# Moving the high part of each weight slot by 128 bytes in a 14-stage float32 kernel on one core

## The chip, the cores and the metric

The kernel runs on one core of a Trainium2 chip. The metric is the device time of one execution in microseconds (us). Before the change it is 2582.13 us, the median of 3 runs (2581.76 to 2582.37). Smaller is better.

## The reference

The program takes 256 tokens of width 1024 through two blocks, 14 stages in all. Every stage ends with a residual sum and a layer norm. All arithmetic is float32. Cut to what matters here:

```python
def first_block(x, ...):                 # two layers
    for layer in range(2):
        h = hybrid_mixer(x, ...)         # x @ w_in, gating, gated linear attention, @ w_out
        x = layer_norm(ALPHA * x + h, ...)
        f = swiglu(x, ...) if layer % 2 == 0 else moe_swiglu(x, ...)   # 8 experts, top 2
        x = layer_norm(ALPHA * x + f, ...)

def second_block(x, mem, ...):           # two layers
    for i in range(2):
        x = layer_norm_2(ALPHA * x + 0.5 * swiglu_2(x, gate, up, down), ...)
        x = layer_norm_2(ALPHA * x + (mixer_ab if i % 2 == 0 else mixer_c)(x, ...), ...)
        x = layer_norm_2(ALPHA * x + memory_attn(x, mem, ...), ...)
        x = layer_norm_2(ALPHA * x + 0.5 * swiglu_2(x, gate, up, down), ...)
```

`swiglu(x)` is `(silu(x @ w_gate) * (x @ w_up)) @ w_down`. Nearly all the arithmetic is products of the 256 tokens with large weight matrices.

## The kernel before, in words

**Split products.** Outside the expert stage, each float32 product is made of three products of float32r tiles. A value is split into a high part (rounded) and a low part (the rest). `product` (lines 581 to 583) issues them in this order: stationary high with moving high, stationary high with moving low, stationary low with moving high. I call such a group of three a triple.

**Two ways round.** In a plain block the tokens are the stationary operand (128 x 128) and the weights stream past as the moving operand, 512 columns at a time. The page writes it `bank<-part_hi,x_hi`, moving operand first. In a turned block the weights are stationary and 256 tokens are moving: `bank<-x_hi,turned_part_hi`. The stationary operand of a plain block is `x_hi`/`x_lo` (the stage's input), `cat_hi`/`cat_lo` (input of an output projection), `hT_hi`/`hT_lo` (hidden units of a feed-forward) or `mem_hi`/`mem_lo`.

**The ring.** Weights pass through a ring of 9 slots in SBUF. A slot holds one block of 128 x 2048 float32 as it arrives (`raw`, 8192 bytes of each partition), and beside it another 8192 bytes. ScalarE rounds the block into the second half (`part_hi`, line 548). VectorE then subtracts and writes the low part over the raw block (`part_lo`, line 556). TensorE reads both parts. For a turned block the same slot is used through a second set of views, whose names begin with `turned_`. In the expert stage (the middle of the program) there is no split: each half of a slot holds raw weights, `raw` and `raw_hi`, and plain float32 matmuls read them as the moving operand (lines 1203, 1217, 1250, 1272).

**Order.** The order of the work on each engine is written out by hand. Slots are given out by the order in which earlier blocks are used up (`Ring.place`); the three mixers with their own buffers above slot 6 use slots 0 to 5 only. In the first stage the blocks 0, 1, 2, 3 of `w_in` lie in slots 0, 1, 2, 3, and TensorE takes 12 matmuls (4 triples) from a slot before it goes to the next.

**Addresses.** `x_at` is the address of `x_hi`, a multiple of 128 bytes. `place_memory` puts each view at the next address that stands in a chosen relation to it modulo 128 (`at_place`).

Of the kernel before, what the change touches and what calls it, by code (L numbers as in the profile page):

```python
# [5 lines left out]
P = 128  # L6
F32 = mybir.dt.float32
F32R = mybir.dt.float32r
# [38 lines left out]
SLOT = 2048  # L47
LINE = 128
APART = 64
# [89 lines left out]
class Program:  # L139
# [34 lines left out]
    def place_memory(self):  # L174
        nc = self.nc
        base = (nc.sbuf_base + 31) // 32 * 32
        at = [base]
# [7 lines left out]
        def over(name, shape, dt, offset):  # L185
            return nc.alloc_sbuf_tensor_at(name, shape, dt, offset=offset)

        x_at = at[0] = (at[0] + LINE - 1) // LINE * LINE
# [26 lines left out]
        self.vstats = put("gating_stats", [P, TT, GM_HEADS, 8])  # L215
        self.att_stats = put("softmax_stats", [P, 16, 3, TT])
        self.raw, self.part_hi, self.part_lo, self.raw_hi = ([[], []] for _ in range(4))
        at[0] = (at[0] + LINE - 1) // LINE * LINE
        for i in range(RING):
            if i == MIX_RING:  # L220
                arena = at[0]
            raw_at, hi_at = at[0], at[0] + 4 * SLOT + APART
            at[0] = hi_at + 4 * SLOT + APART
            for name, turned in (("", 0), ("turned_", 1)):
                at_place = lambda first: first + (x_at + turned * APART - first) % LINE
                self.raw[turned].append(over(f"{name}raw{i}", [P, SLOT], F32, at_place(raw_at)))
                self.part_lo[turned].append(over(f"{name}part_lo{i}", [P, SLOT], F32R, at_place(raw_at)))
                self.raw_hi[turned].append(over(f"{name}raw_hi{i}", [P, SLOT], F32, at_place(hi_at)))
                self.part_hi[turned].append(over(f"{name}part_hi{i}", [P, SLOT], F32R, at_place(hi_at)))
        at[0] = (at[0] + LINE - 1) // LINE * LINE  # L230
        silu_at = at[0]
        self.silu = [put(f"silu{i}", [P, FC]) for i in range(2)]
        self.h = [put(f"h{i}", [P, FC]) for i in range(2)]
# [2578 lines left out]
```

## Time and profile before

| | |
|---|---|
| median of 3 runs | 2582.13 us |
| the profiled execution, its own time | 2579.98 us |
| its span, first to last instruction | 2578.7 us |
| TensorE matmul busy | 2524.8 us, 98% |
| TensorE weight load busy | 1788.1 us |
| VectorE, ScalarE, GpSimd busy | 1054.1, 820.6, 144.4 us |
| HBM traffic | 248 GB/s over the span |
| granted TensorE clock, mean | 0.996 |

A matmul row's duration covers its way through the array, so neighbouring matmuls overlap. The duration is not what one matmul costs in a row of them. The distance from the start of one to the start of the next is, and the timeline gives starts to 0.01 us. Over several triples that resolves a nanosecond or two of each.

### The profile page before, as it was taken

What the parts mean: (1) busy time and instruction counts of PE and PEld (TensorE: products, weight loads), DVE (VectorE), ACT (ScalarE), POOL (GpSimd) and SP (SyncE); (2) the same over time, 40 slices, a digit from 0 to 9 for tenths busy, and PEclk for the clock granted to TensorE, in tenths of its full rate; (3) what the DMA queues carried; (4) which work ended last, traced back from release to release, by engine and by line L of the source; (5) the groups of instructions that cost most, each with busy time, mean ns of one, the idle gap of its engine ahead of it and who ended that gap; (6) DMA issues with size and microseconds to landing.
All of it is one profiled execution on the core that took longest, in us unless ns stands there. A gap on an engine that the chain in (4) does not pass through costs nothing.

```text
span 2578.7 us, 40653 instructions
## 1 busy us (share of the span) xinstructions
PE 2524.8 (98%) x18155; PEld 1788.1 (69%) x18155; DVE 1054.1 (41%) x1488; ACT 820.6 (32%) x1138; POOL 144.4 (6%) x143
## 2 busy tenths in 40 slices
PE   8999999999999999999999999999999999899998
PEld 6899885444444444444448987797988988688897
DVE  5755562010101000010116558646546545655554
ACT  5444342110101101010114436454444444634442
POOL 2200120000000000000000001000000004400000
PEclk9999999999999999999999999999999999999999
DMA  7565458999999999999985544446546546264651
GB/s 259 199 214 188 161 212 338 371 360 382 380 361 370 393 375 356 376 390 355 377 297 193 188 142 147 142 153 212 196 163 197 195 158 250 69 210 164 216 187 55
DMA packets 335286, 641.51 MB, mean 249 GB/s; under 512 B 15620, under 2 KB 128432, under 8 KB 334976
## 3 DMA queue, kind: packets, MB, share of 16 engines
q1 hardware_dynamic: 330000, 618.64, 66.5%
q0 software_dynamic: 5104, 20.20, 2.3%
q8 instruction: 144, 2.36, 0.4%
q14 instruction: 38, 0.31, 0.0%
HBM read 637.72 MB, written 1.05 MB: 248 GB/s over the span
## 4 chain that ended last, share of the span: by engine, by line
PE 91%; DVE 4%; POOL 2%; ACT 1%; DMA 1%; issue 0%; SPq 0%; DVEq 0%
PE bank L581 17%; PE bank L583 17%; PE bank L582 17%; PE bank L1203 15%; PE bank L1217 8%; PE bank L1250 7%; PE bank L1272 4%; DVE part_lo L556 1%; PE bank L977 1%; PE bank L1235 1%; PE bank L948 1%; PE bank L593 1%; POOL bias L2488 1%; PE bank L1189 1%; DVE x_rows L1833 1%; ACT part_hi L548 1%
## 5 line engine op out<-in xcount | busy, mean ns | idle before, releaser
L556 DVE TENSOR_TENSOR part_lo<-raw,part_hi 128x2048 fp32r<-128x2048 f32 x153 | 348.3, 2291 | 169.5 <-ACT part_hi L548 169.3
L581 PE MATMUL bank<-x_hi,turned_part_hi 128*128 128x256 f32 x1440 | 401.4, 279 | 0.0
L583 PE MATMUL bank<-x_hi,turned_part_lo 128*128 128x256 f32 x1440 | 399.1, 277 | 0.0
L582 PE MATMUL bank<-x_lo,turned_part_hi 128*128 128x256 f32 x1440 | 398.8, 277 | 0.0
L548 ACT ACTIVATE part_hi<-raw 128x2048 fp32r<-128x2048 f32 x153 | 289.1, 1908 | 14.9 <-DMA raw<-in_mem_w_kv_dram 6.9
L581 PEld LDWEIGHTS bank<-x_hi,turned_part_hi 128*128 128x128 f32 x1440 | 270.5, 188 | 4.1 <-issue 1.0
L582 PEld LDWEIGHTS bank<-x_lo,turned_part_hi 128*128 128x128 f32 x1440 | 270.3, 188 | 3.4
L583 PEld LDWEIGHTS bank<-x_hi,turned_part_lo 128*128 128x128 f32 x1440 | 270.8, 188 | 0.0
L556 DVE TENSOR_TENSOR turned_part_lo<-turned_raw,turned_part_hi 128x2048 fp32r<-128x2048 f32 x98 | 223.4, 2310 | 90.5 <-ACT turned_part_hi L548 89.9
L1203 PE MATMUL bank<-raw,expert_in 128*64 128x512 f32 x896 | 214.1, 598 | 0.0
L581 PE MATMUL bank<-part_hi,x_hi 128*128 128x512 f32 x528 | 213.2, 404 | 0.6 <-DVE x_lo L1781 0.5
L1203 PE MATMUL bank<-raw_hi,expert_in 128*64 128x512 f32 x896 | 211.2, 592 | 0.0
L2332 DVE TENSOR_TENSOR h<-silu,bank 128x256 f32<-128x256 f32 x56 | 23.6, 421 | 457.9 <-ACT silu L1742 457.9
L583 PE MATMUL bank<-part_hi,x_lo 128*128 128x512 f32 x528 | 208.4, 395 | 0.0
L582 PE MATMUL bank<-part_lo,x_hi 128*128 128x512 f32 x528 | 208.2, 394 | 0.0
L548 ACT ACTIVATE turned_part_hi<-turned_raw 128x2048 fp32r<-128x2048 f32 x98 | 183.3, 1908 | 4.6 <-DMA turned_raw<-in_c_w_in_dram 4.0
L581 PE MATMUL bank<-part_hi,hT_hi 128*128 128x512 f32 x440 | 173.1, 393 | 1.2 <-DVE hT_lo L1781 0.9
L582 PE MATMUL bank<-part_lo,hT_hi 128*128 128x512 f32 x440 | 172.6, 392 | 0.0
L583 PE MATMUL bank<-part_hi,hT_lo 128*128 128x512 f32 x440 | 172.5, 392 | 0.0
L1384 ACT ACTIVATE silu<-bank 128x256 f32<-128x256 f32 x110 | 42.3, 385 | 361.2 <-PE bank L583 361.2
L1203 PEld LDWEIGHTS bank<-raw_hi,expert_in 128*64 128x64 f32 x896 | 64.2, 137 | 128.0 <-issue 128.0
L2341 DVE TENSOR_TENSOR h<-silu,bank 128x128 f32<-128x128 f32 x56 | 16.1, 287 | 332.0 <-ACT silu L1752 332.0
(272 smaller groups left out, 3505.5 us busy)
## 6 DMA issues: line engine op xcount, KB each, us to landing
raw<-in_exp_w_gate_dram SPq DMA_DIRECT2D x112, 512.0 KB, 6.3
raw<-in_exp_w_up_dram SPq DMA_DIRECT2D x112, 512.0 KB, 7.2
raw_hi<-in_exp_w_gate_dram SPq DMA_DIRECT2D x112, 512.0 KB, 8.0
raw_hi<-in_exp_w_up_dram SPq DMA_DIRECT2D x112, 512.0 KB, 8.7
raw<-in_exp_w_down_dram SPq DMA_DIRECT2D x56, 1024.0 KB, 12.2
raw_hi<-in_exp_w_down_dram SPq DMA_DIRECT2D x56, 1024.0 KB, 13.7
raw<-in_ffn_w_down_dram SPq DMA_DIRECT2D x55, 1024.0 KB, 5.0
turned_raw<-in_ffn_w_gate_dram SPq DMA_DIRECT2D x70, 512.0 KB, 4.2
```

Of the source, the lines that this page charges most:

```text
L548: p.nc.scalar.activation(p.part_hi[t][i][:, :], p.raw[t][i][:, :], ACT.Copy).then_inc(*self.rounded.step((name,)))
L556: p.nc.vector.tensor_tensor(p.part_lo[t][i][:, :], p.raw[t][i][:, :], p.part_hi[t][i][:, :].bitcast(F32), ALU.subtract).then_inc(*self.spl ...
L581: nc.tensor.matmul(out, stat_hi, move_hi, start=start, stop=False, skip_group_check=True)
L582: nc.tensor.matmul(out, stat_hi, move_lo, start=False, stop=False, skip_group_check=True)
L583: return nc.tensor.matmul(out, stat_lo, move_hi, start=False, stop=stop, skip_group_check=True)
L593: mm = nc.tensor.transpose(p.bank[bank][:, k * P:(k + 1) * P], src[:, k * P:(k + 1) * P], p.const("identity"))
L948: mm = nc.tensor.matmul(p.bank[4 + i % 2][:, qt * T:(qt + 1) * T], q[:, qt * P:(qt + 1) * P], k, start=(j == 0), stop=(j == len(terms) - 1 ...
L1203: mm = p.nc.tensor.matmul(p.bank[4][half * PAIR:(half + 1) * PAIR, :].rearrange("p (m n) -> p m n", m=2), xe[:, kk, 0:PAIR], w[:, k, :, ha ...
L1217: mm = p.nc.tensor.matmul(p.bank[5][f * FOUR:(f + 1) * FOUR, 0:256].rearrange("p (m n) -> p m n", m=2), xe[:, kk, PAIR:SLOTS], w[:, k, :, ...
L1250: mm = p.nc.tensor.matmul(p.bank[0][half * PAIR:(half + 1) * PAIR, :], p.hT[:, j, d * PAIR:(d + 1) * PAIR], w[:, j, half * 512:(half + 1) ...
L1272: mm = p.nc.tensor.matmul(p.bank[1][f * FOUR:(f + 1) * FOUR, 0:256], p.hT[:, 2, tile * FOUR:(tile + 1) * FOUR], w[:, j, f * 256:(f + 1) * ...
L1384: nc.scalar.activation(p.silu[k % 2][:, :], p.bank[4 + k % 2][:, 0:FC], ACT.Silu).then_inc(*p.s.step(("silu", st, k)))
```

## The change

The number of instructions, their kinds, shapes and order are the same on every engine. Only start addresses of the unturned `raw_hi` and `part_hi` views change. Per slot, with A the slot's first address (slot i begins at A0 + 16512 i, before and after):

| view | before | after |
|---|---|---|
| `raw`, `part_lo` | A | A |
| `raw_hi`, `part_hi` | A + 8320 | A + 8192 |
| `turned_raw`, `turned_part_lo` | A + 64 | A + 64 |
| `turned_raw_hi`, `turned_part_hi` | A + 8256 | A + 8256 |

So before, the plain views were 65 lines of 128 bytes apart and the turned ones 64; after, both are 64. All else in memory stays where it was. Worked out from the allocation, counted in lines of 128 bytes: A0 = 63104 is line 493, so A is an odd line in the slots 0, 2, 4, 6, 8 and an even line in 1, 3, 5, 7. The stationary operands `x_hi`, `x_lo`, `cat_hi`, `cat_lo`, `mem_hi`, `mem_lo` begin at odd lines (`x_hi` at 16512 is line 129), `hT_hi` and `hT_lo` at even ones, and each 128 x 128 block in them begins a multiple of 512 bytes further on.

```diff
-        at[0] = (at[0] + LINE - 1) // LINE * LINE
+        at[0] += (x_at - at[0]) % LINE
         for i in range(RING):
             if i == MIX_RING:
                 arena = at[0]
-            raw_at, hi_at = at[0], at[0] + 4 * SLOT + APART
-            at[0] = hi_at + 4 * SLOT + APART
-            for name, turned in (("", 0), ("turned_", 1)):
-                at_place = lambda first: first + (x_at + turned * APART - first) % LINE
-                self.raw[turned].append(over(f"{name}raw{i}", [P, SLOT], F32, at_place(raw_at)))
-                self.part_lo[turned].append(over(f"{name}part_lo{i}", [P, SLOT], F32R, at_place(raw_at)))
-                self.raw_hi[turned].append(over(f"{name}raw_hi{i}", [P, SLOT], F32, at_place(hi_at)))
-                self.part_hi[turned].append(over(f"{name}part_hi{i}", [P, SLOT], F32R, at_place(hi_at)))
-        at[0] = (at[0] + LINE - 1) // LINE * LINE
+            for turned, name in enumerate(("", "turned_")):
+                raw_at = at[0] + turned * APART
+                hi_at = raw_at + 4 * SLOT
+                self.raw[turned].append(over(f"{name}raw{i}", [P, SLOT], F32, raw_at))
+                self.part_lo[turned].append(over(f"{name}part_lo{i}", [P, SLOT], F32R, raw_at))
+                self.raw_hi[turned].append(over(f"{name}raw_hi{i}", [P, SLOT], F32, hi_at))
+                self.part_hi[turned].append(over(f"{name}part_hi{i}", [P, SLOT], F32R, hi_at))
+            at[0] += 8 * SLOT + LINE
         silu_at = at[0]
```

`P` is 128, `SLOT` 2048 elements, `LINE` 128 and `APART` 64 bytes.

## Rows read from the trace of the kernel before

**Rows 1.** The page, the chain that ended last, by engine.
```profile
PE 91%; DVE 4%; POOL 2%; ACT 1%; DMA 1%; issue 0%; SPq 0%; DVEq 0%
```
**Rows 2.** Stretches before, in and behind the expert stage: length, then busy by engine.
```profile
0.00:420.00 420.00, 403.51 (x2412) 345.80 (x2413) 248.97 (x367) 186.75 (x199) 61.13 (x65) 1.00 0.63 216
420.00:1370.00 950.00, 947.72 (x8442) 412.11 (x8437) 103.70 (x216) 100.83 (x247) 2.29 (x4) 1.00 0.96 363
1370.00:2578.70 1208.70, 1173.55 (x7307) 1030.19 (x7306) 701.42 (x906) 533.02 (x692) 81.02 (x75) 0.99 0.51 170
```
**Rows 3.** Timeline of TensorE, first stage, slot 0 then slot 1: start, duration (us).
```profile
27.43 0.39 PE L581 MATMUL bank<-part_hi,x_hi 128*128 128x512 f32 x1
...
30.17 0.40 PE L581 MATMUL bank<-part_hi,x_hi 128*128 128x512 f32 x1
...
32.96 0.39 PE L581 MATMUL bank<-part_hi,x_hi 128*128 128x512 f32 x1
```
**Rows 4.** Timeline, output projection of the first stage: slots 1 and 5.
```profile
98.75 0.40 PE L581 MATMUL bank<-part_hi,cat_hi 128*128 128x512 f32 x1
98.99 0.40 PE L582 MATMUL bank<-part_lo,cat_hi 128*128 128x512 f32 x1
...
103.65 0.39 PE L581 MATMUL bank<-part_hi,cat_hi 128*128 128x512 f32 x1
```
**Rows 5.** Matmuls of line 581, by tile: duration in ns, min/median/max.
```profile
L581 PE MATMUL bank<-x_hi,turned_part_hi x1440: 276/276/469, 43.2 to 2529.0; 128*128 128x256 f32 x180
L581 PE MATMUL bank<-part_hi,x_hi x528: 387/393/776, 13.8 to 2562.6; 128*128 128x512 f32 x176
L581 PE MATMUL bank<-part_hi,hT_hi x440: 387/392/502, 124.1 to 2569.5; 128*128 128x512 f32 x147
L581 PE MATMUL bank<-part_hi,cat_hi x192: 388/393/628, 86.0 to 2383.4; 128*128 128x512 f32 x192
L581 PE MATMUL bank<-part_hi,mem_hi x64: 390/393/477, 1678.2 to 2318.5; 128*128 128x512 f32 x64
```
**Rows 6.** Timeline, first and last of 3,504 evenly running 512-column matmuls.
```profile
19.35 0.39 PE L582 MATMUL bank<-part_lo,x_hi 128*128 128x512 f32 x1
...
2569.76 0.39 PE L582 MATMUL bank<-part_lo,hT_hi 128*128 128x512 f32 x1
```
**Rows 7.** Timeline, feed-forward down product, slot 6 both times, 207 and 216 us.
```profile
207.50 0.39 PE L581 MATMUL bank<-part_hi,hT_hi 128*128 128x512 f32 x1
207.72 0.40 PE L582 MATMUL bank<-part_lo,hT_hi 128*128 128x512 f32 x1
...
210.24 0.28 PE L581 MATMUL bank<-x_hi,turned_part_hi 128*128 128x256 f32 x1
...
216.58 0.40 PE L581 MATMUL bank<-part_hi,hT_hi 128*128 128x512 f32 x1
...
218.68 0.28 PE L581 MATMUL bank<-x_hi,turned_part_hi 128*128 128x256 f32 x1
```
**Rows 8.** Timeline, turned block, 256 moving columns.
```profile
43.70 0.28 PE L581 MATMUL bank<-x_hi,turned_part_hi 128*128 128x256 f32 x1
...
45.74 0.28 PE L581 MATMUL bank<-x_hi,turned_part_hi 128*128 128x256 f32 x1
```
**Rows 9.** Matmuls of the expert stage, line 1203, the same columns.
```profile
L1203 PE MATMUL bank<-raw,expert_in x896: 592/592/645, 409.8 to 1338.5; 128*64 128x512 f32 x180
L1203 PE MATMUL bank<-raw_hi,expert_in x896: 592/592/593, 411.5 to 1340.2; 128*64 128x512 f32 x180
```
**Rows 10.** VectorE's subtraction, plain and turned, the same columns.
```profile
L556 DVE TENSOR_TENSOR part_lo<-raw,part_hi x153: 2277/2291/2618, 10.9 to 2534.9; 128x2048 fp32r<-128x2048 f32 x153
L556 DVE TENSOR_TENSOR turned_part_lo<-turned_raw,turned_part_hi x98: 2282/2291/3106, 30.4 to 2502.0; 128x2048 fp32r<-128x2048 f32 x98
```
**Rows 11.** ScalarE's rounding, plain and turned, the same columns.
```profile
L548 ACT ACTIVATE part_hi<-raw x153: 1897/1906/1971, 8.9 to 2532.6; 128x2048 fp32r<-128x2048 f32 x153
L548 ACT ACTIVATE turned_part_hi<-turned_raw x98: 1895/1905/1947, 28.4 to 2499.7; 128x2048 fp32r<-128x2048 f32 x98
```

## The prediction

> **What bounds the kernel now.** I read the busy shares first, then the chain, then the stretches, and last the starts of single matmuls. TensorE is busy 2524.8 of 2578.7 us (the table of the profile above), and the chain that ended last lies on it for 91% of the span [rows 1]. So a nanosecond on each of some thousand matmuls reaches the end almost undiminished. The three stretches [rows 2] show it idle for 16.5 us before the expert stage (420.00 - 403.51), 2.3 us in it and 35.2 us behind it. In the last stretch ScalarE and VectorE are busy 533 and 701 of 1,209 us: there is room if TensorE gets a few us faster.
>
> The change moves no instruction. It can act only through the time that an instruction takes at another address. The reader should therefore look for rows that differ in nothing but address, and there are some.
>
> **Does the address matter at all?** Take the start-to-start time of a triple of 512-column matmuls. In the first stage, slot 0 gives 4 triples in 30.17 - 27.43 = 2.74 us, 685 ns each; slot 1 gives 4 in 32.96 - 30.17 = 2.79 us, 697.5 ns each [rows 3]. In the output projection, slots 1 and 5 give 7 in 103.65 - 98.75 = 4.90 us, 700 ns each [rows 4]. Same shapes, same order, same clock; the slots differ in the parity of their 128-byte line. I name two classes by the lines that stand in front: class A, where the low part has the same parity as the stationary operand and the high part the other one (`x`, `cat`, `mem` with even-numbered slots, `hT` with odd-numbered); class B, the reverse. Counting the blocks gives 712 triples in A and 512 in B, 1,224 in all, which is 528 + 440 + 192 + 64 [rows 5].
>
> From all starts between the two in [rows 6] I averaged the triples without a gap in them: A 689.4 ns (629 of them), B 695.6 (452), both 692.0. That is the steady cost at stake: 1,224 x 0.692 = 847 us, a third of the span.
>
> The pattern also depends on what ran before. Slot 6 with `hT`, class B, runs 4 triples in 210.24 - 207.50 = 2.74 us (685 ns) at one place and 3 in 2.10 us (700 ns) nine microseconds later [rows 7]. The same addresses give either. A line-581 matmul with both operands in the same parity takes 0.22 us in the fast pattern (207.50 to 207.72) and 0.24 in the slow one (98.75 to 98.99, [rows 4]); at the trace's full resolution the three of a triple take 226, 234, 226 and 236, 234, 230 ns. I read this as two streams, the moving operand and the load of the next stationary block, that run in lockstep and settle into patterns that collide more or less often.
>
> **The change part by part.**
>
> *Matmuls of plain blocks, 3 x 1,224.* Before, the moving operand's parity goes high, low, high = 0,1,0 or 1,0,1. After, high and low have the same parity. Class A becomes "same as the stationary operand in all three" (712), class B "other in all three" (512). No 512-column triple of the trace runs in either way, so this is the unknown cost, bounded by the nearest rows. From below: turned blocks have constant parity in both operands and do 6 triples of 256 columns in 45.74 - 43.70 = 2.04 us, 340 ns each [rows 8]; twice the columns at that rate is 680 ns. Then 1,224 x (680 - 692.0) = -14.7 us. The shortest durations say nearly the same: 387 against a median of 393 and 392 [rows 5], some 6 ns a matmul, 18 a triple, -22 us if every one were the shortest; but only 340 ns is seen to last, so I take -14.7 as the end. From above: 700 ns, the slowest pattern that repeats [rows 4, 7], on every triple: 1,224 x (700 - 692.0) = +9.8 us.
>
> Between them I go by position, the nearest evidence there is. Over the 3,504 intervals of [rows 6], a line-581 matmul takes 233.0 ns where moving and loaded operand have the same parity and 230.4 where they differ; line 582 takes 229.2 and 232.2; line 583 takes 230.6 and 229.7. The change turns the high part alone, lines 581 and 583. A triple of class A goes from differing to same there: +2.6 + 0.9 = +3.5 ns, x 712 = +2.5 us. A triple of class B goes the other way: -3.5 x 512 = -1.8 us. The sum is +0.7 us. The two classes nearly cancel because the change swaps relations rather than removing one.
>
> *Turned blocks, 1,440 + 128 triples and more.* Their four views don't move. Nothing, except that a changed phase at their start may carry over for a triple or two.
>
> *Expert stage.* `raw_hi` moves by 128 bytes. These matmuls take 592 ns at the median whether they read `raw` or `raw_hi`, and whichever the slot; min and median agree [rows 9]. No sensitivity is to be seen, so 0 for 950 us of the span. The transfers carry the same bytes in the same packets to partitions that stay, and I count 0 for them.
>
> *VectorE and ScalarE.* The subtraction reads both halves of a slot at once, and here the trace has both distances: plain (8320 bytes apart) 2291 ns at the median, turned (8192 apart) 2291 [rows 10]. The rounding has 1906 and 1905 [rows 11]. The minima of the subtraction differ by 5 ns, x 153 = 0.8 us of an engine that is busy 41%. Cost 0; TensorE hides it. If that cover were gone it would be under 1 us.
>
> The sum is +0.7 us on the profiled execution's own 2579.98 us, that is 2580.7. This execution was 2.15 us under the median of the runs, so on the median's scale it is 2582.13 + 0.7 = 2582.8 us. A difference of under 0.2%, 5.2 us, is what can't be told from no change here; that is 4.2 ns per triple.
>
> **The rivals.**
>
> *Faster: constant parity lets the streams settle at the floor.* For it: turned blocks, with constant parity whichever the slot, run at 340 ns mostly (their median duration is their minimum, 276, [rows 5]), while plain blocks rarely run at theirs. And class B's good pattern [rows 7] is made of 226, 234 and 226 ns, where the 226s are the two matmuls with the same parity: the same relation three times could be 3 x 226.7 = 680. Against it: turned blocks have their stationary operand 64 bytes off the moving one modulo 128, plain ones have 0, and lines 581 and 583 are, on average, not faster with same parity. If all settle: -14.7 us, 2567.4. If class A alone reaches 680: 712 x (680 - 689.4) = -6.7 us, 2575.4.
>
> *Slower: same parity locks in the slow pattern.* In slots 1 and 5 [rows 4] the matmuls with same parity take 236 and 230 ns, the one with other parity 234. After, 712 triples have same parity throughout, and once in such a pattern nothing shifts them out of it, since each step is like the last. At 700 for class A: 712 x (700 - 689.4) = +7.5 us, 2589.7; for both classes +9.8, 2591.9. It decides as soon as the mean triple passes 692.0 + 4.2 = 696.2 ns.
>
> *The address plays no part.* The Trainium skill says in "TensorE: Matmul & The Clock Gate", section "Step-by-step: what each phase is for", that loading the next tile's weights does not take SBUF bandwidth from the running matmul, as both have their own read port. By that rule the change would cost 0.0 and the time be 2582.1. The trace speaks against it: with one shape, the triple takes 685 in slot 0 and 697.5 in slot 1 [rows 3]. The result would be in the same bracket as my forecast, so I can't tell them apart by the time alone, but by the triples' pattern after.
>
> **How the numbers follow.** No measurable change, by cancelling or because addresses play no part: 0.42, of it 0.05 for the latter. The streams settle lower, over 5.2 us faster: 0.33. They lock higher, over 5.2 us slower: 0.25. The likeliest is the first, its own range 2577 to 2588. The full range reaches into both rivals: down to 2570, short of the floor for all, as that would take both classes; up to 2592, the slow pattern for all.
>
> **What would show it right or wrong.** Right: slots of both parities still show triples between 686 and 700, the mean stays within 688 to 696, and the lines 556, 548 and 1203 keep 2291, 1906 and 592 ns. Wrong: a long row of equal intervals at 226 to 227 (floor) or above 233 (lock) in the timeline of plain blocks; the mean duration of the 512-column matmuls then moves from 393 toward 388 or 397. It would be wrong in its ground, too, if the turned blocks or the expert stage changed, since their places are the same or without effect.

## The result, and the profile after

The changed kernel takes 2592.24 us against 2581.76 for the kernel before on the same chip, each the median of 7 runs; one of the seven, at 7315 us with a granted clock of 0.34, enters no ratio below, and the other six have a median of 2591.65. The ratio is 1.0044, 95% interval [1.0034, 1.0054]: slower by 0.44%, some 11.4 us. The forecast was 2582.8 with a range of 2570 to 2592; 2592.24 lies 0.24 us above that range and 2591.65 lies 0.35 us inside it, so the parts below have to say what went wrong, not the number. The profiled executions have spans of 2591.8 and 2578.7 us.

The chain of the kernel after, by engine, answers to [rows 1]. It still lies on TensorE:

```profile
PE 92%; DVE 5%; ACT 1%; issue 1%; POOL 0%; DMA 0%; SPq 0%; DVEq 0%
```

The stretches of the kernel after (length, then busy us of TensorE, its weight load, VectorE, ScalarE and GpSimd, granted clock, DMA share, GB/s), to be held against [rows 2]:

```profile
0.00:420.00 420.00, 402.76 (x2363) 346.76 (x2367) 248.65 (x366) 186.50 (x199) 61.21 (x65) 1.00 0.63 216
420.00:1371.00 951.00, 948.74 (x8483) 412.13 (x8483) 102.52 (x213) 101.11 (x248) 2.14 (x3) 1.00 0.96 363
1371.00:2591.80 1220.80, 1185.52 (x7315) 1043.20 (x7313) 699.99 (x910) 533.30 (x692) 80.22 (x75) 0.99 0.50 168
```

Read three things here. The granted clock is 1.00, 1.00 and 0.99 of full speed (the 2.4 GHz level) in both kernels, so the clock is no cause. TensorE's idle time behind the expert stage is 1220.80 - 1185.52 = 35.3 us, before 35.2: no new wait. And it is busy 1185.5 us there instead of 1173.6, for nearly the same matmuls (7315 against 7307, as the stretches are cut by time). The time is inside the instructions.

The rows by tile, kernel after (duration in ns, min/median/max; first and last start), answer to [rows 5, 9, 10, 11]:

```profile
L580 PE MATMUL bank<-x_hi,turned_part_hi x1440: 276/281/469, 43.5 to 2541.9; 128*128 128x256 f32 x180
L580 PE MATMUL bank<-part_hi,x_hi x528: 387/392/776, 14.2 to 2575.6; 128*128 128x512 f32 x176
L580 PE MATMUL bank<-part_hi,hT_hi x440: 388/392/504, 124.8 to 2582.6; 128*128 128x512 f32 x147
L1202 PE MATMUL bank<-raw,expert_in x896: 592/592/644, 412.5 to 1341.3; 128*64 128x512 f32 x180
L1202 PE MATMUL bank<-raw_hi,expert_in x896: 592/592/593, 414.3 to 1343.0; 128*64 128x512 f32 x180
L555 DVE TENSOR_TENSOR part_lo<-raw,part_hi x153: 2279/2292/2294, 9.8 to 2547.8; 128x2048 fp32r<-128x2048 f32 x153
L547 ACT ACTIVATE part_hi<-raw x153: 1895/1904/1965, 7.8 to 2545.5; 128x2048 fp32r<-128x2048 f32 x153
```

(The file is one line shorter: 581, 556, 548 and 1203 are now 580, 555, 547 and 1202.) The one row that moved is the one whose addresses did not: matmuls of turned blocks have a median of 281 instead of 276 ns. The moved plain blocks have 392 instead of 393 and 392. The expert matmuls, the subtraction (2292, was 2291) and the rounding (1904, was 1906) stand still. From first to last start of line 1202 it is 412.5 to 1343.0, 930.5 us; before it was 409.8 to 1340.2, 930.4. So of 13.1 us, 2.7 were lost ahead of the expert stage and 10.3 behind it.

Both programs have the same 18,155 matmuls in the same order, so the start-to-start times of the two traces can be subtracted one by one:

| part | change, us |
|---|---|
| turned blocks, 4,704 matmuls | +12.3 |
| plain blocks, 3,672 matmuls | -1.5 |
| other products of the three lines (256 columns) | -0.1 |
| expert stage | 0.0 |
| all other TensorE work, with its waits | +2.0 |
| first matmul's start | +0.3 |

The sum is 13.0, against 13.1 between the two spans. The 2.0 lies at the score, weighing and turning matmuls of the attention and at the turned `x_rows`, where TensorE waits for ScalarE and VectorE. In six other kernels below with the same instructions the same item is between -0.7 and +1.6, so it is scatter rather than an effect.

What a turned run looks like now: the timeline of TensorE in the kernel after (start, duration, us), a plain block with `hT` and the run of turned triples behind it:

```profile
192.54 0.39 PE L580 MATMUL bank<-part_hi,hT_hi 128*128 128x512 f32 x1
...
194.58 0.39 PE L580 MATMUL bank<-part_hi,hT_hi 128*128 128x512 f32 x1
194.81 0.39 PE L581 MATMUL bank<-part_lo,hT_hi 128*128 128x512 f32 x1
195.03 0.39 PE L582 MATMUL bank<-part_hi,hT_lo 128*128 128x512 f32 x1
195.26 0.28 PE L580 MATMUL bank<-x_hi,turned_part_hi 128*128 128x256 f32 x1
195.37 0.28 PE L581 MATMUL bank<-x_lo,turned_part_hi 128*128 128x256 f32 x1
...
199.14 0.28 PE L580 MATMUL bank<-x_hi,turned_part_hi 128*128 128x256 f32 x1
```

Plain: 4 triples in 195.26 - 192.54 = 2.72 us, 680 ns each. Turned: 11 triples in 199.14 - 195.26 = 3.88 us, 353 ns each, where [rows 8] had 340. The pattern holds over the whole run of 16 triples, across its change of slot. Over all evenly running turned triples the mean is 351.8 ns (343.7 before), and 12% of them are at 345 or less (74% before). There are two patterns, 340 and 353, and next to nothing between. They don't go with the slot that is read: 11% of the triples of even slots and 14% of those of odd slots are fast. Below, a turned run is such a row of turned triples between two plain blocks. It is fast when it is at 340 and slow when it is at 353.

The plain blocks, slot 0 then slot 1 in the first stage of the kernel after, answer to [rows 3]:

```profile
28.42 0.39 PE L580 MATMUL bank<-part_hi,x_hi 128*128 128x512 f32 x1
...
30.46 0.40 PE L580 MATMUL bank<-part_hi,x_hi 128*128 128x512 f32 x1
...
32.56 0.39 PE L580 MATMUL bank<-part_hi,x_hi 128*128 128x512 f32 x1
```

3 triples in 2.04 us (680) and 3 in 2.10 (700). As a shorthand I write the parities of high part, low part and, behind the stroke, stationary operand: 1 for an odd 128-byte line and 0 for an even one. The means are:

| class | before | after |
|---|---|---|
| A, high part moves into the same parity | 01/1 689.2, 10/0 689.7 | 11/1 685.3, 00/0 683.5 |
| B, high part moves into the other parity | 10/1 696.2, 01/0 694.3 | 00/1 698.3, 11/0 700.3 |

Class A went down by some 5 ns and class B up by some 3, and over 712 and 512 triples the two nearly cancel, to -1.5 us.

### The profile page after: what moved, and what is told of

The parts are those of the page before. It is cut to its first block, busy times and chain, and to the rows that moved or that the text cites. A ratio compares the mean times of both kernels' runs of the same rounds, so it can differ in the third digit from the quotient of the medians.

```text
span 2591.8 us, 40653 instructions
## 1 busy us (share of the span) xinstructions
PE 2537.0 (98%) x18155; PEld 1802.1 (70%) x18155; DVE 1051.2 (41%) x1488; ACT 820.9 (32%) x1138; POOL 143.6 (6%) x143
## 4 chain that ended last, share of the span: by engine, by line
PE 92%; DVE 5%; ACT 1%; issue 1%; POOL 0%; DMA 0%; SPq 0%; DVEq 0%
PE bank L580 17%; PE bank L582 17%; PE bank L581 17%; PE bank L1202 15%; PE bank L1216 8%; PE bank L1249 7%; PE bank L1271 4%; DVE part_lo L555 2%; PE bank L1234 1%; PE bank L976 1%; PE bank L592 1%; PE bank L947 1%; DVE x_rows L1832 1%; PE bank L1188 1%; PE bank L960 1%; DVE stats L1812 1%
## 5 line engine op out<-in xcount | busy, mean ns | idle before, releaser
L547 ACT ACTIVATE part_hi<-raw 128x2048 fp32r<-128x2048 f32 x153 | 289.1, 1907 | 13.3 <-DMA raw<-in_mem_w_kv_dram 7.1
L547 ACT ACTIVATE turned_part_hi<-turned_raw 128x2048 fp32r<-128x2048 f32 x98 | 183.2, 1906 | 4.1 <-DMA turned_raw<-in_c_w_in_dram 3.9
```

The source lines that it names most:

```text
L547: p.nc.scalar.activation(p.part_hi[t][i][:, :], p.raw[t][i][:, :], ACT.Copy).then_inc(*self.rounded.step((name,)))
```

## The experiments

Main theory: a row of float32r triples has a phase between its two streams (the moving operand and the load of the next stationary block); the addresses of a plain block decide which one it leaves behind, and a run of turned triples keeps it until something breaks it. First rival: what the turned run inherits is not a phase, but some lasting state that goes with the slots' places. Second: the addresses of the turned blocks themselves matter in the new layout. Each figure is the median of its runs, and each ratio is to the kernel before on the same chip, which had 2579.19, 2579.9, 2580.54 and 2580.17 us in the four batches. Counts of runs and means of triples are from one profiled execution of each kernel.

**A break ahead of each turned run (nudge_after).** One small matmul without a use, of other widths in the five feed-forward stages.

```diff
+NUDGE = {1: 16, 4: 32, 7: 48, 8: 64, 11: 96}
+        if by_tiles(q) and NUDGE.get(st):
+            p.nc.tensor.matmul(p.bank[6 + k % 2][0:32, 0:NUDGE[st]], p.x_hi[:, 0, 0:32], p.x_hi[:, 0, 0:NUDGE[st]],
+                               start=True, stop=True, skip_group_check=True)
```

> The changed kernel with one extra small float32r matmul (32 stationary columns, result unused) in front of each of the 70 turned runs of the five feed-forwards; its moving width is 16, 32, 48, 64, 96 columns in stages 1, 4, 7, 8, 11. No address changes. Handover: the extra matmul shifts the phase, so in some of the stages all turned runs flip from 353 to 340 ns a triple (14 runs x 16 x 13.3 ns = 3.0 us a stage), in others they stay; which widths do it isn't known. Cost 70 x 0.03 to 0.1 us = 2 to 7 us. Layout rival: no stage flips, and the time is 2594 to 2599.

Measured 2583.49 us, ratio 1.0018 [1.0008, 1.0027], some 7 us under the changed kernel's ratio. Its timeline, the same place as above:

```profile
194.41 0.39 PE L583 MATMUL bank<-part_hi,hT_lo 128*128 128x512 f32 x1
194.64 0.17 PE L826 MATMUL bank<-x_hi 128*32 128x16 f32 x1
194.67 0.36 PE L581 MATMUL bank<-x_hi,turned_part_hi 128*128 128x256 f32 x1
...
195.11 0.28 PE L581 MATMUL bank<-x_hi,turned_part_hi 128*128 128x256 f32 x1
...
199.87 0.28 PE L581 MATMUL bank<-x_hi,turned_part_hi 128*128 128x256 f32 x1
```

14 triples in 4.76 us, 340 ns. All 70 runs of the feed-forward stages are fast, with any width (turned mean 342.5). No address was changed, so neither the slots' places nor the turned blocks' addresses force the 353: it was inherited, and one instruction ends it.

**One half of the change undone (undo_odd, undo_even).** The high part of the odd slots, or of the even ones, goes back to its other parity.

```diff
-                hi_at = raw_at + 4 * SLOT
+                hi_at = raw_at + 4 * SLOT + (LINE if i % 2 and not turned else 0)
```

and `i % 2 == 0` for the other.

> The change is undone in the odd-numbered slots alone (their plain high part is back at A + 8320); even-numbered slots keep A + 8192. Theory (handover): a turned run of matmuls keeps the phase with which the plain matmuls before it end, 340 ns a triple or 353. In the kernel before, hT blocks in odd slots (0.72 of them) ended so that the turned run behind went at 340; after the change they end in another phase and it goes at 353. Undone there, the turned runs behind odd slots go back to 340, those behind even slots stay at 353: some 45 of 70 feed-forward runs x 16 triples x 13.3 ns = -9.6 us, plain triples +2 -1 us, so about 2583 to 2585. Rival (layout): the turned views are slow because of what lies 8192 bytes apart in the ring, whatever ran before: the turned triples then fall by the slot they read, not by what ran before them, and the time is about halfway, 2587.

> The change is undone in the even-numbered slots alone. Handover: turned runs behind odd slots stay at 353, as after the change; those behind even slots (about 25 of 70) go as in the kernel before, half 340 and half 353: -2.7 us. Plain x, cat, mem triples in even slots 685 -> 689, +1.7 us, hT in even slots 700 -> 694, -0.9 us. Sum 2590. Layout rival: 2587, and turned triples that read even slots at 340.

undo_odd: 2575.78 us, 0.9986 [0.9977, 0.9996], better than expected. undo_even: 2587.83 us, 1.0032 [1.0019, 1.0044]. That is nearer to the 2587 of the layout rival than to my 2590, but the rival's other sign is missing: of the turned triples that read even slots 20% are fast, of the others 28%. By the same subtraction against the kernel before, undo_odd has turned blocks at -1.3 and plain ones at -6.2 us, undo_even +10.1 and -1.7. The timeline of undo_odd at the same place:

```profile
192.88 0.39 PE L580 MATMUL bank<-part_hi,hT_hi 128*128 128x512 f32 x1
...
193.34 0.40 PE L582 MATMUL bank<-part_hi,hT_lo 128*128 128x512 f32 x1
193.58 0.28 PE L580 MATMUL bank<-x_hi,turned_part_hi 128*128 128x256 f32 x1
...
193.93 0.28 PE L580 MATMUL bank<-x_hi,turned_part_hi 128*128 128x256 f32 x1
...
198.69 0.28 PE L580 MATMUL bank<-x_hi,turned_part_hi 128*128 128x256 f32 x1
```

The last plain matmul takes 0.24 us to the first turned one (0.23 in the slow case above), the first turned triple 0.35, and the next 14 take 340 each (4.76 us). Medians over all turned runs agree: at the border a fast one has 235 and 122 ns, a slow one 226 and 117. So some 9 + 5 ns more pass where plain meets turned, or they don't; I call that a slip of the phase. Sorted by the class that ran last, the 70 turned runs of a kernel that stand directly behind a down product are:

| class ahead of the turned run | kernels | turned runs fast/slow |
|---|---|---|
| 10/0 | before, undo_odd | 45/2, 47/0 |
| 01/0 | before, undo_even | 13/10, 13/10 |
| 00/0 | after, undo_even | 0/47, 0/47 |
| 11/0 | after, undo_odd | 3/20, 23/0 |

The last line shows why undo_odd beat its expectation: I had taken the class 11/0 for slow because it was so in the kernel after. It is fast here. So the last class alone doesn't decide; what ran ahead of it does too.

What that is can be read off the traces. In the feed-forward stages 65 turned runs of 16 triples stand behind another turned run, with four plain triples (half a down product) in between. Over the six kernels with 64 bytes of offset and no added or cut matmul (before, after, undo_odd, undo_even, and two that follow, all_same and undo_odd_hT) the pattern behind follows from the class in between and the pattern ahead, for all 390 runs:

| class in between | behind it, with 340 ahead | behind it, with 353 ahead |
|---|---|---|
| 10/0 | 340 (86) | 340 (4) |
| 10/1 | 340 (35) | 340 (10) |
| 01/0 | 353 (20) | 340 (20) |
| 11/0 | 340 (20) | 353 (20) |
| 00/0 | none | 353 (90) |
| 11/1 | 353 (15) | 353 (70) |

So 11/0 hands on what it finds. In the kernel after all these rows are at 353, since 00/0 leaves 353 behind whenever it comes; in undo_odd they are all at 340, since 10/0 leaves 340. This is a sorting of traces that were there already; no kernel was made to test it.

The odd slots with `x` gained in undo_odd: 10/1 has 689.7 where the kernel before had 696.2.

**All plain blocks in the same parity (all_same).** All slots on odd lines, `hT` and `x` too.

```diff
-            at[0] += 8 * SLOT + LINE
+            at[0] += 8 * SLOT + 2 * LINE
-        at[0] += 9216
+        at[0] += 8448
```

(and one small table laid over another to make room; `hT` and the small buffers around it move along).

> The changed kernel with slots 16640 bytes apart instead of 16512, so that every slot begins at an odd 128-byte line, and hT at odd lines too (two statistics tiles share a place and a late buffer is 768 bytes smaller to make room). Every plain triple then has high, low and stationary operand of the same parity. Theory: they all run at 680 to 685 ns, where the changed kernel has 684 for 712 triples and 699 for 512: -7.5 us. Turned runs all start in the phase that gives 353: no change. 2584 to 2586, with turned triples at 352. Rival: what makes the turned runs slow is the mixture of the two classes; then they go back to 340 and the time is 2573.

2583.41 us, 1.0017 [1.0007, 1.0027], as expected. Its timeline:

```profile
190.81 0.40 PE L581 MATMUL bank<-part_hi,hT_hi 128*128 128x512 f32 x1
...
191.51 0.40 PE L581 MATMUL bank<-part_hi,hT_hi 128*128 128x512 f32 x1
...
192.20 0.39 PE L581 MATMUL bank<-part_hi,hT_hi 128*128 128x512 f32 x1
...
192.88 0.39 PE L581 MATMUL bank<-part_hi,hT_hi 128*128 128x512 f32 x1
...
193.56 0.28 PE L581 MATMUL bank<-x_hi,turned_part_hi 128*128 128x256 f32 x1
...
195.68 0.28 PE L581 MATMUL bank<-x_hi,turned_part_hi 128*128 128x256 f32 x1
```

The plain triples take 700, 690, 680, 680 ns: they settle at the floor within two triples and stay. The turned ones behind take 353 each (6 in 2.12 us). By subtraction: plain -10.8 us, turned +12.6. The two effects of the change are now apart: the same parity everywhere is worth nearly 11 us on the plain blocks, and costs more than that on the turned ones.

**Both together, with small matmuls (all_same_nudge), and small matmuls in the kernel before (before_nudge).**

```diff
+def pe_nudge(p, bank, x):
+    p.nc.tensor.matmul(bank[0:32, 0:16], x[:, 0, 0:32], x[:, 0, 0:16], start=True, stop=True, skip_group_check=True)
+        if by_tiles(q):
+            pe_nudge(p, p.bank[6 + k % 2], p.x_hi)
```

> All slots and hT on odd lines (as all_same), and one small matmul (32 stationary, 16 moving columns, result unused) in front of each turned run of the feed-forwards, behind the two transposes in their first tile, and in front of the turned blocks of the mixers. Handover: all_same measured 2583.4 with its turned triples at 352 and its plain ones at 683. The 70 feed-forward runs flip to 340: 70 x 16 x 13.3 ns = -14.9 us, the small matmuls cost 70 x 28 ns = +2.0 us, the mixers' blocks give -1 to -2 us. 2568 to 2571, under the kernel before and undo_odd (2575.8). Rival (the gains don't add, since the small matmul disturbs the plain runs' fast pattern too): 2574 to 2578.

> The kernel before with the same small matmul in front of each of the 70 turned runs of the feed-forwards, nothing else. Handover: 58 of these runs were fast already and can only lose the 28 ns; 12 flip: 70 x 0.028 - 12 x 0.213 = -0.6 us, no measurable change. Rival (the small matmul helps in another way, whatever the phase, as it did by 8.8 us in the changed kernel): 5 to 9 us faster.

The cut shows the place in the feed-forwards; all_same_nudge has the small matmul at the mixers' turned blocks too, 93 in all, before_nudge 70. all_same_nudge: 2577.85 us, 0.9994 [0.9985, 1.0003]; both kinds of block are in their fast pattern (683.2 and 341.6, 89% of the turned triples fast), but the time missed its expectation by 7 us and more. It lies where the rival had it, 2574 to 2578, though not for the rival's reason, as the plain blocks kept their 683. before_nudge: 2584.23 us, 1.0017 [1.0008, 1.0026], a miss too. Its timeline shows the reason:

```profile
178.36 0.39 PE L583 MATMUL bank<-part_hi,hT_lo 128*128 128x512 f32 x1
178.59 0.17 PE L613 MATMUL bank<-x_hi 128*32 128x16 f32 x1
178.62 0.37 PE L581 MATMUL bank<-x_hi,turned_part_hi 128*128 128x256 f32 x1
178.82 0.28 PE L582 MATMUL bank<-x_lo,turned_part_hi 128*128 128x256 f32 x1
178.94 0.28 PE L583 MATMUL bank<-x_hi,turned_part_lo 128*128 128x256 f32 x1
```

The small matmul takes 0.03 us, which is what I had counted. But the next one then takes 0.20 to its successor instead of 0.12. That is 0.11 us each, half of the 16 x 13.3 ns = 0.21 us that a flipped run is worth, and a plain loss where the run was fast already. In before_nudge 70 x 0.11 us less 10 flipped runs of 0.21 is +5.6 us, where the ratio says +4.4. My reading is that the weights' load finds too little running time to hide under; that was not tested by itself.

**The turned blocks' offset (apart0, apart32).** The turned views lie 64 bytes behind the plain ones modulo 128; here 0 and 32.

```diff
-APART = 64
+APART = 0
```

> The changed kernel with the turned views at A instead of A + 64: stationary and moving operand of the turned blocks then stand at the same place modulo 128 as those of the plain blocks do. The changed kernel's plain runs end in one phase nearly always, so all turned runs start alike. If 64 bytes are what lets them have a fast pattern at all, every turned triple takes 353 or more, and the time is 2592 to 2602. If the offset plays no part, the share of fast triples stays near 0.12 and the time 2592. A shift of half a pattern would give fast runs: 2580.

> The same with the turned views at A + 32. If the offset adds to the phase with which a turned run starts, 32 bytes put it elsewhere than 64 and 0 do, and the share of fast triples changes from 0.12 to near 1 or 0. If it plays no part, 0.12 and 2592 us.

One run each: 2599.0 and 2600.45 us, with 2579.9 for the kernel before. The timeline of apart0:

```profile
43.86 0.28 PE L580 MATMUL bank<-x_hi,turned_part_hi 128*128 128x256 f32 x1
...
46.74 0.28 PE L580 MATMUL bank<-x_hi,turned_part_hi 128*128 128x256 f32 x1
```

8 triples in 2.88 us, 360 ns each. The means are 358.0 and 356.5, and not one turned triple is fast, where 12% are with 64 bytes. So the second rival is right to this extent: the turned addresses matter. That they say which patterns there are, and not which is taken, is my reading; whether a small matmul would bring out the fast pattern at 0 or 32 bytes was not tested.

**A break that costs nothing (split).** all_same, with the last 512-column matmul of a down product in two pieces, of other widths in each stage.

```diff
+SPLIT = {1: 256, 4: 264, 7: 272, 8: 240, 11: 248}
+    nc.tensor.matmul(out[:, 0:w], stat_lo, move_hi[:, 0:w], start=False, stop=stop, skip_group_check=True)
+    return nc.tensor.matmul(out[:, w:512], stat_lo, move_hi[:, w:512], start=False, stop=stop, skip_group_check=True)
```

> all_same with the last 512-column matmul in front of each of the turned runs (65 of 70) issued as two of w and 512 - w columns, the same sums; w is 256, 264, 272, 240, 248 in stages 1, 4, 7, 8, 11. A cheaper shift than the extra matmul, which cost 28 ns before it and some 85 ns behind it, as the next 128-column load isn't covered. Handover: where the split leaves another phase than 226.7-ns steps do, a stage's turned runs flip to 340 at no cost, up to 65 x 0.213 = -13.8 us against all_same's 2583.4, so 2570 if all flip; w = 256 may keep the phase (2 x 113.3) and its stage stay at 353. Rival (only a break in the row of matmuls, as with the extra one, changes the pattern): no stage flips, 2583.4.

2575.81 us, 0.9979 [0.9969, 0.9988]. The timeline in the stage with 256, then in the one with 264:

```profile
160.25 0.28 PE L595 MATMUL bank<-part_hi,hT_lo 128*128 128x256 f32 x1
160.37 0.28 PE L596 MATMUL bank<-part_hi,hT_lo 128*128 128x256 f32 x1
160.48 0.28 PE L581 MATMUL bank<-x_hi,turned_part_hi 128*128 128x256 f32 x1
...
161.90 0.28 PE L581 MATMUL bank<-x_hi,turned_part_hi 128*128 128x256 f32 x1
...
1417.96 0.28 PE L595 MATMUL bank<-part_hi,hT_lo 128*128 128x264 f32 x1
1418.08 0.28 PE L596 MATMUL bank<-part_hi,hT_lo 128*128 128x248 f32 x1
...
1418.55 0.28 PE L581 MATMUL bank<-x_hi,turned_part_hi 128*128 128x256 f32 x1
...
1419.91 0.28 PE L581 MATMUL bank<-x_hi,turned_part_hi 128*128 128x256 f32 x1
```

Behind an even split the turned triples take 1.42 / 4 = 355 ns, behind an uneven one 1.36 / 4 = 340. Of the turned runs behind a split, 48 are at 340; the 12 at 353 are those of the stage with 256. The split itself costs about 0.01 us (0.12 + 0.12 for 0.226). Eight columns are enough, in either direction (240, 248, 264 and 272 all do it), and no address differs from all_same; that speaks for a phase and against a matter of addresses.

**undo_odd with `hT` in the other parity (undo_odd_hT).** The small buffers around `hT` move by the same 128 bytes.

```diff
-                hi_at = raw_at + 4 * SLOT
+                hi_at = raw_at + 4 * SLOT + (LINE if i % 2 and not turned else 0)
+        at[0] += LINE
```

> undo_odd with hT_hi and hT_lo (stationary operand of the down products, 880 of the plain matmuls' 3,672... 440 triples) moved up by 128 bytes, to odd lines. Weight views, plain and turned, stay as in undo_odd. Handover: the down products in even slots have the same parity in all operands, as in all_same, end in steps of 226 and send the turned runs behind them into 353, those in odd slots end as x triples of class 10/1 did in undo_odd, after which 4 of 5 turned runs were slow. Turned share at 340 falls from 0.82 to 0.2 to 0.4: +9 us, plain triples 698 -> 684 in even slots x 152 = -2 us: 2581 to 2584. Layout rival: turned blocks' times don't depend on where hT lies; 2573.5.

2576.44 us, 0.9989 [0.998, 0.9999], faster than expected: of the runs behind 10/1, 46 are fast and 6 slow, where I had expected 4 of 5 slow. Those behind 11/1 are slow as elsewhere (all 23). By subtraction plain -7.7 us, turned +2.3.

**The cheap break in the changed kernel (after_split), and in all_same at every place (best).**

```diff
+            mm = product_split(p.nc, SPLIT, *operands) if tt and half else product(p.nc, *operands)
```

`SPLIT` is 264; best has the same in the two other functions that end ahead of a turned run.

> The changed kernel, all addresses as they are in it, with the last 512-column matmul in front of 65 turned runs issued as 264 + 248 columns. Handover: the 43 runs or so behind down products of class 00/0 (same parity) flip as in split's stages with w other than 256, those behind class 11/0 (other parity) may or may not; 43 to 65 x 0.213 = -9 to -14 us against the changed kernel's 2592.2, so 2578 to 2583, no slower than the kernel before. Layout rival: 2592, since no address differs from the changed kernel.

> split with w = 264 in all stages, and the same split at the last matmul of every down product of the other tiles and of every plain block of the mixers (second token tile). Against split's 2575.8: the 12 runs of stage 1 flip, -2.6 us, the 5 first runs -1 us, the mixers' turned blocks of 32 to 64 triples that started slow behind a plain block -2 us. 2570 to 2572. Rival: a split inside a row of plain blocks throws the plain matmuls behind it out of their 680-ns pattern, 683 -> 690 on half of 800 triples = +3 us: 2573 to 2575.

after_split: 2586.4 us, 1.0025 [1.0016, 1.0035], a miss. The runs behind 11/0 became fast (20), but the 40 behind 00/0 stayed slow, so the split isn't a break that works at any phase. best: 2571.94 us, 0.9971 [0.9959, 0.9982], faster than both kernels by 7.5 and some 19 us (the latter from the two ratios, 2580.17 x (1.0044 - 0.9971)). Its timeline:

```profile
192.40 0.39 PE L593 MATMUL bank<-part_hi,hT_hi 128*128 128x512 f32 x1
...
192.86 0.28 PE L595 MATMUL bank<-part_hi,hT_lo 128*128 128x264 f32 x1
192.97 0.28 PE L596 MATMUL bank<-part_hi,hT_lo 128*128 128x248 f32 x1
193.09 0.28 PE L581 MATMUL bank<-x_hi,turned_part_hi 128*128 128x256 f32 x1
193.44 0.28 PE L581 MATMUL bank<-x_hi,turned_part_hi 128*128 128x256 f32 x1
...
198.20 0.28 PE L581 MATMUL bank<-x_hi,turned_part_hi 128*128 128x256 f32 x1
```

A first turned triple of 0.35, then 14 in 4.76 us: 340. All 75 runs behind a split are fast; plain triples average 685.0, turned ones 341.7.

## Why the prediction was wrong

**The step that failed** is the one on the turned blocks: "Nothing, except that a changed phase at their start may carry over for a triple or two." The pattern carries over for all 16 triples of a run, and it cost +12.3 us, nearly the whole loss of 13.1. Had it been a triple or two, it would have been at most 2/16 of that, 1.5 us. I had the parts in hand: I wrote that the pattern depends on what ran before [rows 7], and that once in a pattern "nothing shifts them out of it, since each step is like the last", but applied it to the plain blocks alone. Turned blocks are the purest case of equal steps, and the 26% of turned triples in the kernel before that were not at 340 were the sign: their second pattern was there to be read and priced. 1,568 x (353 - 343.7) = +14.6 us was the bound that the range lacked. The prediction had named a change of the turned blocks as the sign that its ground was wrong, and that sign came.

**Plain blocks**: the sum was near (+0.7 predicted, -1.5 measured), but by luck, since both of its terms had the wrong sign. By position I had class A at +3.5 ns and B at -3.5; measured is about -5 for A (689.4 to 684.6) and +3 to +4 for B (695.6 to 699). A mean by position over mixed patterns says nothing of a pattern that repeats; the argument in the faster rival, "three times could be 3 x 226.7 = 680", did. all_same shows it for the plain blocks of all slots (683.1 on average, -10.8 us). Class B went to 700, the bound from above. The cancelling between the classes is real. The mean plain triple is 691 in the kernel after, inside the 688 to 696 that were to show the forecast right: whoever had looked at the plain blocks alone would have seen nothing wrong.

**Expert stage, VectorE and ScalarE** at 0: right (930.5 and 930.4 us; 2292 and 1904 ns), as far as one profile each can tell.

**The rivals.** "Faster" was half right: class A settled, but its gain was eaten by class B. "Slower" gave 2591.9 for both classes, next to the measured 2592.24, by a mechanism that is refuted: same parity is the fast pattern, not the slow one. A number that fits is no proof of its story. "The address plays no part" fell with the result itself, since before and after differ in addresses alone, and again with undo_odd, at 0.9986 [0.9977, 0.9996] against 1.0044 [1.0034, 1.0054]. (undo_even, at 1.0032, is too near to say.) The Trainium skill goes further than the sentence that I weighed: "SBUF — State Buffer", section "Who interferes with whom", has TensorE never waiting on anyone. If that is taken to cover TensorE's own two streams, all the kernels with the same instructions would take one time. No run here shows another engine in TensorE's way at SBUF, but its own triples cost 680 or 700 ns, and 340, 353 or on average 358, by where they read and by what ran ahead.

**The uncertainty.** I could have known that the turned share was the open end, as 4,704 of 8,424 product matmuls were taken at 0 without a range.

## What to carry to other kernels

Where a stream of equal instructions runs in one of two patterns, price a change by what it leaves behind for the next stream as well as by its own part, and bound every stream that can inherit, the unmoved ones above all. Look for the second pattern in the kernel before: a median that equals the minimum hides a quarter of slow cases, so take shares, not medians. If a stream is stuck in the slow pattern, an uneven cut of one instruction ahead of it may free it for some 0.01 us; an added small matmul costs ten times that. Try it before relying on it: behind one class of addresses, 00/0, the cut freed none.

## What the runs showed of the hardware

- Triples of float32r matmuls with 128 x 128 stationary blocks ran at 680 or 700 ns (512 columns) and 340 or 353 (256 columns) at the same full clock, each repeating itself over several triples. All operands of the plain ones on lines of one parity: 683.1 on average.
- Every run of 16 turned triples between two plain blocks kept its pattern to its end, but for the first two triples. It was left where another kind of block, a small matmul or a cut of 264/248 came in between, not with a cut of 256/256. One exception: the one row of 64 turned triples went from 353 to 340 halfway, where its third slot begins, in the kernel after and five others, with nothing in between.
- Which pattern four plain triples left behind depended on their class and on the pattern ahead of them, without exception in 390 runs (the table above).
- The 340 pattern of turned blocks was seen only with moving and stationary operand 64 bytes apart modulo 128. At 0 and 32 bytes the means were 358.0 and 356.5 (one run each).
- Open: why 11/0 hands on the pattern that it finds while 01/0 turns it round, why the cut frees runs behind 11/1 and 11/0 but not behind 00/0, and what in the chip the two streams share. That they collide is my reading; the runs show times and addresses, not the collision. The 2.0 us at the attention's waits are called scatter by comparison with other kernels, not by repeated profiles of one.
